# A short first token list and a first expert that begins with 32 tokens, in a two-layer decoder step

## The chip, the cores and the metric

The kernel runs on one core of a Trainium2 chip. The metric is the time of one execution on the device, in microseconds (us). Engines are called PE (matmul), DVE (vector), ACT (activation), POOL and SP; the last two mostly issue DMAs here. PE's clock is granted at one of two levels, 1.2 or 2.4 GHz; the profile writes them as 0.50 and 1.00.

## What is computed

One inference step of a trunk with two layers, over 512 prompt tokens and 64 sample tokens (576 rows of 1024 values). Each layer is a mixer (convolution and attention in layer 0, sparse attention in layer 1) followed by a mixture of 16 experts. The change touches the experts' part alone. Cut to that part:

```python
def hier_moe(h, w_group, b_group, w_router, b_router, w_gate, w_up, w_down):
    g_w, g_idx = lax.top_k(jax.nn.softmax(g_logits, axis=-1), 1)      # one group of four
    top_v, top_i = lax.top_k(e_in, TOP_K_INNER)                       # two experts inside it
    expert_id = g_idx * E_PER_GROUP + top_i
    ...
    for e in range(N_EXPERTS):
        hid = jax.nn.silu(x2 @ w_gate[e]) * (x2 @ w_up[e])
        y = y + combine[:, e:e + 1] * (hid @ w_down[e])
```

Each token goes to 2 of 16 experts; an expert's three matrices are 1024x512, 1024x512 and 512x1024 values of 4 bytes, so 2 MB each.

## The kernel before

**Slots and parts.** The experts are worked in 16 slots. Slots 0 and 1 always hold experts 0 and 1; the others are handed out by how many tokens each expert got. `UNITS` gives each slot's room in units of 32 tokens, 47 units in all. A slot is cut into parts (`PARTS`) of 64 tokens, with a last one of 32 where the number of units is odd. Slot 0 has 3 units: part 0 has 64 tokens, part 1 has 32. A part's place in the sequence is called g. For each g, PE does gate and up (L1306, function `part_features`) and, one part later, down (L1326) of g-1.

**Routing.** After the mixer's output projection, DVE works out each token's expert from the router's scores (`route`, L2109 on). It waits for the scores (`route_mm`), sets `quarter` with four memsets (L2111), finds the two experts of each token, and gives PE a 0/1 mask. PE adds up the places of the tokens in their experts' lists (L1268, L1271, `pos_mm`), and DVE reduces these to `pos_of` (L2154), ten numbers for each partition. Then come the lists: DVE compares `pos_of` with the slot numbers 0 to 127 (`slot_of`, two instructions of 128x640), PE multiplies this by the token numbers (L1277), DVE copies the result to `list16` (L2159), PE spreads the lists of experts 0 and 1 over the partitions (L1281), and DVE writes the row numbers to `tok_u` (L2163). `pos_x` and `slot_x` (a compare of 128x320) serve the places 128 to 159 of a list (L1285). Behind this stand, on DVE and in this order, the rank of the experts (`ranking`, whose last instruction L2174 tells SP which weights to load), the order of the other lists (`list_order`, ending with L2202), and then `inputs(0)`.

**Gathers.** POOL fetches tokens by an indirect DMA for each unit of 32 tokens (L855) from `hn_scratch`, a copy of the normalised rows in DRAM, which POOL itself wrote a little earlier (L780). It waits for the `tok` semaphore and for that copy. `inputs(g)` on DVE turns the gathered rows (L2280) and multiplies them by the gain (L1892, a helper's line that stands for most two-operand instructions). PE waits for this (`xgt`) at the start of each part.

**Weights.** SP streams 48 blocks of 2 MB a layer (L578) into a ring of 7 (layer 0) or 8 (layer 1) places. The first 6 are loaded earlier. From slot 2 on each load waits for `ranked` once, and then for the place that it overwrites: `gate_mm`, `up_mm` or `down_mm` of an earlier slot's last part. ACT issues the DMAs that store each part's output.

## Time and profile before

| | us |
|---|---|
| median of 3 runs | 1408.08 (1398.65 to 1408.93) |
| the profiled execution | 1394.93 |
| its span, first to last instruction | 1393.2 |
| mean granted clock of PE | 0.952 of full |
| PE busy | 1257.5 (90%) |
| DVE busy | 688.6 (49%) |
| ACT busy | 304.7 (22%) |
| POOL busy | 246.7 (18%) |
| mean DMA traffic | 245 GB/s |

The profile is of one execution. 1.7 us of its time lie outside the span. The experts' part of layer 0 runs from about 392 to 660 us, that of layer 1 from about 1096 to 1359 us.

### The profile page before, as it was taken

Reading aid. Unit: us, or ns where it says so; the run is one execution under the profiler, and the core shown is the slowest. Engines: PE = TensorE matmul, PEld = TensorE weight load, DVE = VectorE, ACT = ScalarE, POOL = GpSimd, SP = SyncE. Lnnn points to the kernel's source line nnn. Section 1 sums busy time; section 2 is a strip of 40 time slices with the busy share of each in tenths; the row PEclk is TensorE's granted clock in tenths of the full one; section 3 lists DMA queues with packets and bytes.
Section 4 is the critical chain, followed back from the end, with each engine's and each line's share of the span. In section 5 each row is a group of like instructions: output and inputs, shape, how many; then the busy total and the mean of one; then the engine's idle time right before and its main releaser. Section 6 shows DMA issues by size and latency. Waiting matters only on the chain. (4 is left out here: it accounts for less than half of the span.)

```text
span 1393.2 us, 26984 instructions
## 1 busy us (share of the span) xinstructions
PE 1257.5 (90%) x10555; PEld 705.8 (51%) x10556; DVE 688.6 (49%) x1763; ACT 304.7 (22%) x783; POOL 246.7 (18%) x537
## 2 busy tenths in 40 slices
PE   7999999999779999889599999999999599999890
PEld 3444446554455556455444444555645365555550
DVE  2139954452546443222547897676314645433225
ACT  2121134421201011001213213566602100110012
POOL 1010065001031112100301664000010312111102
PEclk9999999999889999999699998999999799999995
DMA  9443459964479999999501131333342899999966
GB/s 295 144 147 114 155 187 328 333 231 155 167 274 346 393 424 424 424 423 406 164 5 61 35 121 61 122 123 123 126 167 100 310 361 354 425 425 423 422 281 214
DMA packets 88558, 341.05 MB, mean 245 GB/s; under 512 B 26803, under 2 KB 34067, under 8 KB 74466
## 3 DMA queue, kind: packets, MB, share of 16 engines
q1 hardware_dynamic: 67466, 289.49, 54.1%
q0 software_dynamic: 11616, 37.56, 7.5%
q10 hardware_dynamic: 9344, 12.20, 2.5%
q8 instruction: 88, 1.44, 0.4%
q14 instruction: 44, 0.36, 0.1%
HBM read 309.09 MB, written 30.47 MB: 244 GB/s over the span
## 5 line engine op out<-in xcount | busy, mean ns | idle before, releaser
L1306 PE MATMUL banks<-arena 128*32 128x128 f32 (+1 forms) x4736 | 346.5, 333 | 25.5 <-issue 18.2
L1306 PEld LDWEIGHTS banks<-arena 128*32 128x32 f32 (+1 forms) x4736 | 241.9, 126 | 141.4 <-issue 52.8
L1892 DVE TENSOR_TENSOR arena<-arena,banks 128x256 f32<-128x256 f32 (+5 forms) x84 | 38.4, 458 | 382.1 <-PE banks L1306 289.3
L1326 PE MATMUL banks<-arena 128*64 128x512 f32 (+1 forms) x1184 | 173.3, 492 | 1.8 <-ACT arena L1786 1.6
L855 POOL DMA_INDIRECT arena<-hn_scratch,arena x94 | 90.5, 963 | 363.9 <-DVE arena L1892 323.0
L988 PE MATMUL banks<-arena 128*128 128x512 f32 x320 | 142.9, 601 | 0.4 <-DMA arena<-in_wstream 0.4
L1216 PE MATMUL banks<-arena 128*128 128x512 f32 x256 | 114.3, 602 | 3.6 <-ACT arena L1826 2.2
L1016 PE MATMUL banks<-arena 128*128 128x512 f32 x256 | 116.5, 600 | 0.0
L1892 DVE TENSOR_TENSOR arena<-arena 128x256 f32<-128x256 f32 (+13 forms) x220 | 91.1, 433 | 36.5 <-ACT arena L1637 18.2
L1326 PEld LDWEIGHTS banks<-arena 128*64 128x64 f32 (+1 forms) x1184 | 59.8, 124 | 90.3 <-issue 78.5
L1786 ACT ACTIVATE arena<-banks 128x512 f32<-128x512 f32 (+1 forms) x56 | 29.6, 528 | 303.4 <-PE banks L1326 303.4
L988 PEld LDWEIGHTS banks<-arena 128*128 128x128 f32 x320 | 60.2, 193 | 70.2 <-issue 69.8
L2292 DVE STREAM_TRANSPOSE arena<-arena 32x128 f32<-32x128 f32 x304 | 92.0, 303 | 4.9
L2454 DVE SCALAR_TENSOR_TENSOR arena<-arena 128x512 f32<-128x512 f32 x120 | 82.1, 747 | 1.0
L1216 PEld LDWEIGHTS banks<-arena 128*128 128x128 f32 x256 | 48.4, 193 | 62.8 <-issue 59.0
L1892 DVE TENSOR_TENSOR arena<-banks,arena 128x128 f32<-128x128 f32 (+3 forms) x91 | 38.0, 438 | 82.1 <-ACT arena L1708 69.1
L1016 PEld LDWEIGHTS banks<-arena 128*128 128x128 f32 x256 | 46.7, 190 | 56.1 <-issue 54.5
L1796 ACT ACTIVATE arena<-banks 128x256 f32<-128x256 f32 (+1 forms) x56 | 19.6, 349 | 197.4 <-PE banks L1306 191.9
L1574 ACT ACTIVATE arena<-arena 128x1024 f32<-128x1024 f32 (+1 forms) x25 | 26.4, 1056 | 147.8 <-DVE arena L1892 101.7
L1691 ACT ACTIVATE arena<-arena 128x128 f32<-128x128 f32 (+3 forms) x96 | 53.0, 557 | 8.0 <-DVE arena L1938 7.9
L1938 DVE CUSTOM_DVE_ANT_0 arena<-banks,arena 128x128 f32<-128x128 f32 (+3 forms) x96 | 42.7, 482 | 11.4 <-PE banks L1044 7.4
L932 PE MATMUL banks<-arena 128*128 128x128 f32 (+1 forms) x160 | 23.3, 296 | 26.7 <-DVE arena L2348 18.1
(298 smaller groups left out, 1374.7 us busy)
## 6 DMA issues: line engine op xcount, KB each, us to landing
arena<-in_wstream SPq DMA_DIRECT2D x109, 2048.0 KB, 17.2
arena<-in_fox_kt SPq DMA_DIRECT2D x64, 256.0 KB, 4.5
arena<-in_fox_v SPq DMA_DIRECT2D x64, 256.0 KB, 4.2
arena<-in_dsa_page SPq DMA_DIRECT2D x64, 256.0 KB, 4.1
expert_rows<-arena ACTq DMA_DIRECT2D x76, 128.0 KB, 9.4
expert_rows<-arena POOLq DMA_DIRECT2D x1, 6656.0 KB, 19.6
hn_scratch<-arena POOLq DMA_DIRECT2D x8, 512.0 KB, 3.0
expert_rows<-arena ACTq DMA_DIRECT2D x68, 32.0 KB, 7.6
```

The costliest lines, as they stand in the source:

```text
L855: pool.indirect_dma_start(xg[s % 2][:, 256 * w:256 * w + 256], None, rows4, bass.IndirectOffsetOnAxis(tok_u[:, w, s:s + 1], 0))\
L988: last = mm(bank(job % 4), xt[:, c, c0:c1], w[:, c, :], start=(c == 0), stop=(c == DC - 1))
L1016: last = mm(bank(job % 2), xt[:, c, c0:c1], w[:, c, :], start=(c == 0), stop=(c == DC - 1))
L1216: last = mm(bank(out_bank(l, job)), xt[:, c, c0:c1], w[:, c, :], start=(c == first), stop=(c == end))
L1306: last = mm(g3(bank(b, 0, 4 * n, n * j, n * j + n), 4), x[:, c, :], g3(w[:, c, :], 4)[:, :, n * j:n * j + n], start=(c == 0), stop=(c == D ...
L1326: last = mm(bank(3, 0, 8 * n, n * q, n * q + n), ht2[g % 2][:, n * c:n * c + n], w[:, c, 8 * n * q:8 * n * q + 8 * n], start=(c == 0), sto ...
L1691: af(x, x, ACT.Exp, bias=mx[:, c:c + 1], scale=-1.0, accum_out=esum[:, c:c + 1])\
L1786: af(y2[i][:, 0:8 * n], bank(3, 0, 8 * n), ACT.Copy).then_inc(S(f"y_ev{l}"), 1)
L1892: return v.tensor_tensor(out, x, y, op)
L1938: v.tensor_tensor_reduce(sbp[j % 2][a][:, 0:n], bank(a, 0, n), bias(t), -1.0, -TAKEN, ALU.add, ALU.min, mx[:, c:c + 1]).then_inc(S(f"sb{l} ...
L2292: last = v.transpose(g3(ht2[g % 2][p:p + 32, :], 4)[:, :, 32 * half:32 * half + 32], g3(hid2[g % 2][r:r + 32, :], 4)[:, :, 32 * par:32 * p ...
L2454: last = v.scalar_tensor_tensor(out=op, in0=ip, scalar=w, in1=op, op0=ALU.mult, op1=ALU.add)
```

## The change

In words: `CUTS` gives slot 0 the parts of 32 and then 64 tokens; every other slot keeps its parts. A short list, places 0 to 31 of the experts 0 and 1, is made ahead of the whole lists, with a `slot_x` compare of its own, and `tok_u` of the first unit is written from it. POOL waits for the first unit's row numbers and then, separately, for the second's. The four memsets of `quarter` stand behind the mask, and `key` and `pos_x` stand between the steps of the short list.

```diff
-PARTS = tuple((s, 64 * i, min(64, 32 * UNITS[s] - 64 * i)) for s in range(NE) for i in range((UNITS[s] + 1) // 2))
+CUTS = tuple(((0, 1), (1, 2)) if s == 0 else tuple((2 * i, min(2, UNITS[s] - 2 * i)) for i in range((UNITS[s] + 1) // 2))
+             for s in range(NE))
+PARTS = tuple((s, 32 * first, 32 * n) for s in range(NE) for first, n in CUTS[s])
...
+def part_with(s, unit):
+
+    return max(j for j, (first, _) in enumerate(CUTS[s]) if first <= unit)
...
             for s in range(NE):
-                if s in (0, 2):
-                    pool.wait_ge(S(f"tok{l}"), upto(f"tok{l}", s + 2))
+                if s == 2:
+                    pool.wait_ge(S(f"tok{l}"), upto(f"tok{l}", 6))
                 for w in range(UNITS[s]):
+                    if s == 0 and w < 2:
+                        pool.wait_ge(S(f"tok{l}"), upto(f"tok{l}", 2 * w + 2))
                     pool.indirect_dma_start(xg[s % 2][:, 256 * w:256 * w + 256], None, rows4,
...
+            pe.wait_ge(S(f"placed{l}"), upto(f"placed{l}", 1))
+            for n in range(2 * NT):
+                last = mm(bank(5, 0, NE, 0, 32), slot_x[:, n, :], tok_of[:, n, :], start=(n == 0), stop=(n == 2 * NT - 1))
+            last.then_inc(S(f"list_mm{l}"), 1)
+            pe.wait_ge(S(f"tok{l}"), upto(f"tok{l}", 1))
+            mm(bank(6, 0, 2), spread[0:32, 0], list16[0:32, 0:2], start=True, stop=True).then_inc(S(f"list_mm{l}"), 1)
...
-            for w in range(3):
+            for w in range(1, 3):
                 last = mm(bank(6, 2 * w, 2 * w + 2), spread[:, w], list16[:, 0:2], start=True, stop=True)
...
             dve.wait_ge(S(f"tables{l}"), upto(f"tables{l}", 1))
-            for q in range(4):
-                v.memset(quarter[32 * q:32 * q + 32], float(q))
             dve.wait_ge(S(f"route_mm{l}"), upto(f"route_mm{l}", 1))
...
+            tt(slot_x, bc_mid(slot16[:, 0:32], 2 * NT), bc_last(pos_of, 32), ALU.is_equal).then_inc(S(f"placed{l}"), 1)
+            step(v.scalar_tensor_tensor(out=key, in0=cnt, scalar=16.0, in1=kofs, op0=ALU.mult, op1=ALU.add))
+            dve.wait_ge(S(f"list_mm{l}"), upto(f"list_mm{l}", 1))
+            v.tensor_copy(list16[0:32, 0:2], bank(5, 0, 2, 0, 32)).then_inc(S(f"tok{l}"), 1)
+            step(v.tensor_scalar(pos_x, pos_of, -float(CAP), None, ALU.add))
+            dve.wait_ge(S(f"list_mm{l}"), upto(f"list_mm{l}", 2))
+            v.tensor_scalar(tok_u[:, 0, 0:2], bank(6, 0, 2), 4.0, quarter, ALU.mult, ALU.add)\
+                .then_inc(S(f"tok{l}"), 1)
```

How the order of the engines moves. DVE in layer 0, from the reduction to `pos_of` to the one to the rank's first half, before:

```order
L2154 TENSOR_REDUCE arena<-arena 128x10 [waits dve_chain]
L1892 TENSOR_TENSOR arena<-arena 128x640 [waits dve_chain]
L1892 TENSOR_TENSOR arena<-arena 128x640
L2159 CAST arena<-banks 128x16 [waits list_mm]
L2160 TENSOR_SCALAR arena<-arena 128x10
L1892 TENSOR_TENSOR arena<-arena 128x320 [waits dve_chain]
L2163 TENSOR_SCALAR arena<-banks,arena 128x3x2 [waits list_mm]
L2165 SCALAR_TENSOR_TENSOR arena<-arena 128x16
L1892 TENSOR_TENSOR arena<-arena 128x256 [waits dve_chain]
```

The same stretch with the change, where the helper's line is L1908:

```order
L2170 TENSOR_REDUCE arena<-arena 128x10 [waits dve_chain]
L1908 TENSOR_TENSOR arena<-arena 128x320 [waits dve_chain]
L2172 SCALAR_TENSOR_TENSOR arena<-arena 128x16
L2174 CAST arena<-banks 32x2 [waits list_mm,dve_chain]
L2175 TENSOR_SCALAR arena<-arena 128x10
L2177 TENSOR_SCALAR arena<-banks,arena 128x2 [waits list_mm,dve_chain]
L1908 TENSOR_TENSOR arena<-arena 128x640 x2
L2183 CAST arena<-banks 128x16 [waits list_mm]
L1908 TENSOR_TENSOR arena<-arena 128x320
L2186 TENSOR_SCALAR arena<-banks,arena 128x2x2 [waits list_mm]
L1908 TENSOR_TENSOR arena<-arena 128x256
```

The two long compares (128x640) and everything behind them now stand behind a compare, two waits for PE and two small instructions.

PE in layer 0, from the lists to the first expert's matmuls, before:

```order
L1277 MATMUL banks<-arena 128x16 [waits placed]
L1277 MATMUL banks<-arena 128x16 x4
L1281 MATMUL banks<-arena 128x2 [waits tok]
L1281 MATMUL banks<-arena 128x2 x2
L1285 MATMUL banks<-arena 32x16 [waits placed]
L1285 MATMUL banks<-arena 32x16 x9
L1290 MATMUL banks<-arena 128x14 [waits tok]
L1290 MATMUL banks<-arena 128x14 x3
L1291 MATMUL banks<-arena 128x1
L1306 MATMUL banks<-arena 64x256 [waits weights_0,xgt]
```

The same stretch with the change:

```order
L1285 MATMUL banks<-arena 32x16 [waits placed]
L1285 MATMUL banks<-arena 32x16 x9
L1288 MATMUL banks<-arena 128x2 [waits tok]
L1293 MATMUL banks<-arena 128x16 [waits placed]
L1293 MATMUL banks<-arena 128x16 x4
L1293 MATMUL banks<-arena 128x16 [waits placed]
L1293 MATMUL banks<-arena 128x16 x4
L1297 MATMUL banks<-arena 128x2 [waits tok]
L1297 MATMUL banks<-arena 128x2
...
L1307 MATMUL banks<-arena 128x1
L1322 MATMUL banks<-arena 32x128 [waits weights_0,xgt]
```

The short list's eleven matmuls stand first, and the first expert's matmuls are of the 32-token form.

## Rows read from the trace of the kernel before

**Rows 1.** Timeline of layer 0, PE: start us, us, engine, line, what, [idle before <- releaser]

```profile
392.26 12.46 PE L1306 MATMUL banks<-arena 128*64 128x256 f32 x192 [2.17 <-DVE arena L1892]
...
408.14 7.08 PE L1306 MATMUL banks<-arena 128*64 128x256 f32 x64
...
416.89 3.68 PE L1306 MATMUL banks<-arena 128*32 128x128 f32 x128
...
570.36 5.08 PE L1306 MATMUL banks<-arena 128*64 128x256 f32 x32 [5.44 <-issue]
```

**Rows 2.** Windows: us, busy PE, PEld, DVE, ACT, POOL; clock, DMA share, GB/s

```profile
399.00:400.00 1.00, 1.00 (x12) 0.69 (x10) 0.14 (x1) 0.00 (x0) 0.70 (x1) 1.00 0.00 0
459.00:460.00 1.00, 1.00 (x15) 0.49 (x8) 0.94 (x4) 0.38 (x1) 0.00 (x0) 1.00 0.14 57
470.00:655.00 185.00, 172.56 (x1978) 102.46 (x1976) 61.56 (x165) 16.90 (x38) 23.02 (x24) 0.97 1.01 424
```

**Rows 3.** Timeline of layer 0, SP's queue

```profile
389.14 0.35 SPq L578 DMA_DIRECT2D arena<-in_wstream  x1
403.19 0.34 SPq L578 DMA_DIRECT2D arena<-in_wstream  x1
```

**Rows 4.** Timeline of layer 0, the first gathers and inputs

```profile
386.66 1.04 POOL L855 DMA_INDIRECT arena<-hn_scratch,arena  x1 [10.75 <-DVE arena L2163]
...
388.00 0.98 POOL L855 DMA_INDIRECT arena<-hn_scratch,arena  x1 [0.30 <-issue]
...
389.29 0.95 POOL L855 DMA_INDIRECT arena<-hn_scratch,arena  x1 [0.30 <-issue]
...
390.77 0.71 DVE L2280 STREAM_TRANSPOSE arena<-arena 128x512 f32<-128x512 f32 x1 [1.13 <-DMA arena<-hn_scratch,arena]
...
397.10 0.45 DVE L2280 STREAM_TRANSPOSE arena<-arena 128x256 f32<-128x256 f32 x1 [4.58 <-DMA arena<-hn_scratch,arena]
397.57 0.43 DVE L1892 TENSOR_TENSOR arena<-arena 128x256 f32<-128x256 f32 x1
```

**Rows 5.** Timeline of layer 1, the same places

```profile
1090.95 1.02 POOL L855 DMA_INDIRECT arena<-hn_scratch,arena  x1 [10.67 <-DMA hn_scratch<-arena]
...
1095.02 0.71 DVE L2280 STREAM_TRANSPOSE arena<-arena 128x512 f32<-128x512 f32 x1 [1.04 <-DMA arena<-hn_scratch,arena]
...
1096.51 13.60 PE L1306 MATMUL banks<-arena 128*64 128x256 f32 x192 [2.09 <-DVE arena L1892]
```

**Rows 6.** Timeline of layer 0, the start of the routing on DVE

```profile
374.34 0.70 PE L958 MATMUL banks<-arena 128*128 128x20 f32 x4
...
375.03 0.37 DVE L2111 MEMSET arena<- 32x1 f32 x4
375.41 0.24 DVE L1892 TENSOR_TENSOR arena<-banks,arena 128x80 f32<-128x80 f32 x1
```

**Rows 7.** Timeline of layer 0, the lists

```profile
381.84 0.24 DVE L2150 COPY arena<-banks 128x80 f32<-128x80 f32 x1 [0.56 <-PE banks L1271]
...
382.91 1.56 DVE L1892 TENSOR_TENSOR arena<-arena 128x640 f16<-128x640 f16 x2
...
384.86 0.17 DVE L2159 CAST arena<-banks 128x16 f16<-128x16 f32 x1 [0.40 <-PE banks L1277]
...
385.09 0.24 PE L1281 MATMUL banks<-arena 128*128 128x2 f16 x3 [0.27 <-DVE arena L2159]
385.15 0.49 DVE L1892 TENSOR_TENSOR arena<-arena 128x320 f16<-128x320 f16 x1
385.56 0.22 DVE L2163 TENSOR_SCALAR arena<-banks,arena 128x6 uint32<-128x6 f32 x1
...
385.69 0.16 DVE L2165 SCALAR_TENSOR_TENSOR arena<-arena 128x16 f32<-128x16 f32 x1
385.69 0.44 PE L1285 MATMUL banks<-arena 128*32 128x16 f16 x10 [0.36 <-DVE arena L1892]
385.89 0.42 DVE L1892 TENSOR_TENSOR arena<-arena 128x256 f32<-128x256 f32 x1
```

More of the change, by code:

```diff
@@ L68, in part_units @@
 def part_units(s, j):
-    return max(0, min(2, UNITS[s] - 2 * j))
+    return CUTS[s][j][1] if j < len(CUTS[s]) else 0
+def part_with(s, unit):
+    return max(j for j, (first, _) in enumerate(CUTS[s]) if first <= unit)
 ENDS = tuple(sum((u + 1) // 2 for u in UNITS[:s + 1]) for s in range(NE))
@@ L122 @@
     (1, "route_mm mask pos_mm ranked tables turns row_u qbd"),
-    (4, "tok list_mm"),
-    (3, "placed"),
+    (6, "tok list_mm"),
+    (4, "placed"),
     (2, "tail_mm tail_ev route_dve route_act"),
@@ L1287, in route @@
             last.then_inc(S(f"list_mm{l}"), 1)
-            pe.wait_ge(S(f"tok{l}"), upto(f"tok{l}", 3))
+            pe.wait_ge(S(f"tok{l}"), upto(f"tok{l}", 5))
             for w in range(4):
@@ L2148, in route @@
                tokid16[:, 0:NT].unsqueeze(1).unsqueeze(3).broadcast_to([128, 2, NT, NE]), ALU.mult)
+            for q in range(4):
+                v.memset(quarter[32 * q:32 * q + 32], float(q))
             dve.wait_ge(S(f"pos_mm{l}"), upto(f"pos_mm{l}", 1))
@@ L2157, in route @@
                    ALU.is_equal).then_inc(S(f"placed{l}"), 1)
-            dve.wait_ge(S(f"list_mm{l}"), upto(f"list_mm{l}", 1))
+            dve.wait_ge(S(f"list_mm{l}"), upto(f"list_mm{l}", 3))
             v.tensor_copy(list16, bank(5, 0, NE)).then_inc(S(f"tok{l}"), 1)
-            step(v.tensor_scalar(pos_x, pos_of, -float(CAP), None, ALU.add))
             tt(slot_x, bc_mid(slot16[:, 0:32], 2 * NT), bc_last(pos_x, 32), ALU.is_equal).then_inc(S(f"placed{l}"), 1)
-            dve.wait_ge(S(f"list_mm{l}"), upto(f"list_mm{l}", 2))
-            v.tensor_scalar(tok_u[:, 0:3, 0:2], g3(bank(6, 0, 6), 3), 4.0, quarter, ALU.mult, ALU.add)\
+            dve.wait_ge(S(f"list_mm{l}"), upto(f"list_mm{l}", 4))
+            v.tensor_scalar(tok_u[:, 1:3, 0:2], g3(bank(6, 2, 6), 2), 4.0, quarter, ALU.mult, ALU.add)\
                 .then_inc(S(f"tok{l}"), 1)
-            step(v.scalar_tensor_tensor(out=key, in0=cnt, scalar=16.0, in1=kofs, op0=ALU.mult, op1=ALU.add))
             step(tt(g3(square, NE), bc_mid(key, NE), bc_last(key, NE), ALU.is_gt))
@@ L2198, in list_order @@
             v.tensor_copy(order16[:, 0:14], tok_s[:, 0:14])
-            dve.wait_ge(S(f"list_mm{l}"), upto(f"list_mm{l}", 3))
+            dve.wait_ge(S(f"list_mm{l}"), upto(f"list_mm{l}", 5))
             step(tt(tok_x[0:32, :], chosen[0:32, 2, :], bank(7, 0, NE, 0, 32), ALU.mult))
@@ L2204, in other_tokens @@
         def other_tokens(l):
-            dve.wait_ge(S(f"list_mm{l}"), upto(f"list_mm{l}", 4))
+            dve.wait_ge(S(f"list_mm{l}"), upto(f"list_mm{l}", 6))
             v.tensor_scalar(tok_u[:, 4, 2:3], bank(4, 56, 57), 4.0, quarter, ALU.mult, ALU.add)
@@ L2274, in inputs @@
             def inputs(g):
-                s, j = PART_OF[g]
-                n = 32 * part_units(s, j)
+                (s, j), (_, off, n) = PART_OF[g], PARTS[g]
                 name, count = gathered(l, s, j)
                 dve.wait_ge(S(name), upto(name, count))
-                x = xgt[s % 2][:, :, 64 * j:64 * j + n]
-                step(v.transpose(x.rearrange("p c (w i) -> p w c i", i=32), xg[s % 2][:, 512 * j:512 * j + 8 * n]))
+                x = xgt[s % 2][:, :, off:off + n]
+                step(v.transpose(x.rearrange("p c (w i) -> p w c i", i=32), xg[s % 2][:, 8 * off:8 * off + 8 * n]))
                 tt(x, x, bc_last(gain[2 * l + 1], n), ALU.mult).then_inc(S(f"xgt{l}"), 1)
```

8 lines of the change are left out of this document (4 added, 4 removed).

## The prediction

> **What bounds the kernel now.** I read the timeline of PE through the experts of layer 0 first, then the windows of DMA, SP's queue, and last the timeline where the experts start. PE works without a gap from 392.26 us on for most of the phase; a part of 64 tokens takes 7.08 us for gate and up, one of 32 takes 3.68 us, so the time goes with the tokens [rows 1]. Late in the phase PE waits for weights, once for 5.44 us, and comes back slower: 32 matmuls take 5.08 us where half of 7.08, or 3.54, is normal [rows 1]. The windows tell when the weights' stream falls behind. The reader is to see the two empty stretches: no traffic at all at 399 us and a share of 0.14 at 459 us [rows 2]. There the stream had nothing to load, because every place in the ring still held weights that PE needed. From 470 to 655 us, in one window, the DMA share is full [rows 2]. So the end of the phase is set by DMA, but the moment from which DMA runs without rest is set by PE, which frees the places; SP's loads show the same, one at 389.14 us and the next at 403.19, when the first slot's last gate is done [rows 3]. A change of PE's start therefore reaches the end of the layer in full, and a change of the stream's start does not, as long as it is less than the empty time.
>
> What sets PE's start is the chain at the head: DVE ends the order of lists (L2202) 1.13 us ahead of 390.77, so at 389.64, waits for the second gather, transposes at 390.77, multiplies, and PE starts at 392.26 [rows 4]. Layer 1 is alike, with a wait of 1.04 us from 1093.98 to 1095.02, and PE at 1096.51 [rows 5]. So two things have to be early for PE: the gathers that the first part needs, and DVE's way to the end of L2202. The change hastens the first and burdens the second.
>
> **The memsets.** The scores are ready at 375.04, and DVE's memsets run from 375.03 to 375.40; the first work on the scores starts at 375.41 [rows 6]. Without them it can start at about 375.10, so everything behind gains 0.3 us. At their new place they take the same 0.37 us, and DVE waits 0.56 us there for PE's sums [rows 7], which hides them. Without that cover they would cost what they gave.
>
> **The short list.** It stands in front of the whole lists, so its round trip between DVE and PE is paid by all that follows. From the rows of the lists: the compare to PE's first matmul 0.54 us (385.15 to 385.69), PE's ten matmuls 0.44, to DVE's copy 0.04, from the copy to PE's spread 0.23 (384.86 to 385.09), the spread at most 0.24, to `tok_u` 0.04, and 0.13 until the next DVE instruction starts (385.56 to 385.69) [rows 7]. That is 1.66 us. Two small instructions that stood behind now run inside the waits: `pos_x`, 0.2 us between the copy's start and the compare, and `key` (L2165), 0.2 us to the square [rows 7]. Net 1.66 - 0.4 = 1.26 us later, less the memsets' 0.3: about 0.95 us later for the ranking, for the weights' stream, and for L2202. Queued behind this on DVE are the whole lists, the ranking, the order of the lists and both first inputs; PE, POOL and SP wait for them.
>
> **The gathers.** The first row numbers are written about 0.54 + 0.44 + 0.04 + 0.23 + 0.24 + 0.04 + 0.22 = 1.75 us after the compare's start, and that start is 382.91 - 0.3: 384.4. POOL started 0.88 us after L2163's end (385.78 to 386.66) [rows 4, 7], so the first gather starts at about 385.2 in layer 0, where it was 386.66. The second gather was seen by DVE 2.77 us after its start (388.00 to 390.77) [rows 4]; with that the first has landed at 388.0. In layer 1 POOL waited for the copy of the rows, not for the list [rows 5], so the first gather cannot go before about 1090.9 and lands at about 1093.7. The second gather's row numbers now come from the longer way: 385.78 + 0.95 = 386.7, plus 0.88 is 387.6, where it was 388.00; the third then starts near 388.9 instead of 389.29. Nearly unchanged.
>
> **Where the first part starts.** In layer 0 DVE is through with L2202 at 389.64 + 0.95 = 390.6 and the gather has long landed; the wait of 1.13 us goes, and DVE's own work takes its place. In layer 1 it is 1093.98 + 0.95 = 1094.9, again behind the gather. So the inputs start 0.2 us and 0.1 us earlier than before. They are half as large: 0.45 + 0.43 with the small gap is 0.90 us (397.10 to 398.00), against 1.49 us from 390.77 to PE's start, which for the small form is 0.96 with the same 0.06 us hand-over [rows 4]. That is 0.53 us. Sum: 0.7 us earlier in layer 0, 0.65 in layer 1, or 1.35 us in all.
>
> **The second part.** It now needs two gathers and 64 tokens of work on DVE. If the third gather lands 2.8 us after 388.9, at 391.7, the inputs are done at 393.2. PE has 3.68 us of work in the first part at full clock, and more here, since it starts at the low level. The first 192 matmuls took 12.46 us and 13.60 us, where 7.08 + 3.68 = 10.76 is the full-speed time [rows 1, 5]. The excess of 1.70 and 2.84 us is half of the time spent at 1.2 GHz, so the low clock held 3.4 us in layer 0 and 5.7 us in layer 1. A first part of 32 tokens then ends 3.68 + 1.7 = 5.4 us after its start, at about 397.0, almost 4 us after its successor is ready. The new order of sizes costs PE nothing: 32 and 64 tokens make 10.76 us as 64 and 32 did. The first gate place comes free 1.7 us sooner by the sizes alone, 3.4 us of small work ahead of the long gate instead of 6.8 ahead of the short one. That only moves a load into an empty stretch [rows 2, 3]. ACT issues four stores and then two, where it was two and then four.
>
> **The clock.** An earlier start gains in full only if the clock rises earlier by as much. If the rise stays where it is, 0.7 us more at 1.2 GHz is worth 0.35 us. Between the layers the low stretch differs by 2.3 us, worth 1.14 us. I take the full gain, since a later or earlier rise is as likely, and keep 0.35 us a layer for one end and 0.65 + 1.14 = 1.8 us a layer for the other: 0.7 to 3.6 us in all.
>
> **A rule to weigh.** The third gather, started at 389.29 just behind a weights' load at 389.14, was seen by DVE at 397.10, 7.8 us later, while the second, 1.1 us ahead of the load, took 2.8 [rows 3, 4]. With the change the third starts at 388.9 and the load at 389.14 + 0.95 = 390.1, so 1.2 us ahead; I take the short time. The Trainium skill (DMA: Bandwidth & Descriptors, Queues, rings and completion order) says that each DMA engine goes round between its queues packet by packet. By that rule a gather of 128 KB would get a share beside any load and would not wait for the block; this trace speaks against an equal share. By the rule the rival below would have no price at all.
>
> **The rivals.** *The third gather is late after all.* It lands 7.8 us after its start, at 396.7, the 64 tokens take 1.43 us, and the second part is ready at 398.1, 1.1 us after the first ends. Less 0.7 us gained it is +0.4 in layer 0; in layer 1 the third gather starts 2.6 us behind the first at 1090.95, lands at 1101.3 and makes the part ready at 1102.8, while the first part, with 2.84 us of excess, ends at 1095.9 + 6.5 = 1102.4: a wait of 0.4, or -0.25 in all [rows 5]. Together +0.15 us: no change. For it: 1.2 us is a thin lead. Against it: the second gather had the same lead. *Slower: the gap holds the clock down.* The same late gather, and the gap while PE is still at the low level delays the rise; after 5.44 us without work the clock cost 1.54 us on the next 32 matmuls [rows 1]. Adding that to each layer gives 0.15 + 3.1 = +3.3 us. It decides from the point where the third gather lands later than about 395.5. *Slower: the stream.* If the loads were bound from their start, 0.95 us a layer would come on top of the gains' loss, +1.9 us. The empty second at 399 us speaks against it [rows 2]. *The change does nothing:* DVE or the gathers turn out as late as before, since the short list in front costs what it gives; 0.0 us.
>
> **How the numbers follow.** Chances: forecast 0.55 (-0.7 to -3.6 us, likeliest -1.35); nothing gained, by the late gather or by the cost of the list, 0.25; held clock 0.12 (+3.3); the stream 0.08 (+1.9). On the profiled execution the sum gives 1394.93 - 1.35 = 1393.6. The median shown is 13.2 us above that execution, and the three runs spread over 10.3 us, much more than any case here. I carry the difference to the median: 1408.08 - 1.35 = 1406.7. The range has to hold this spread: the profiled execution and one run stand at 1395 and 1399, two at 1408 and 1409. From 1394.93 to 1408.93 + 3.3, cut a little at the upper end, is 1395 to 1411. About 1% (14 us) is what a measurement of this kernel can tell from no change. No case comes near it; 0.02 each way is left for what the runs' own spread can do, 0.96 for the same.
>
> **What would show it.** Right: the first work on the scores at once behind PE's end; POOL's first gather of layer 0 some 1.4 us earlier and that of layer 1 not; L2202's counterpart about 0.95 us later; no wait of DVE for the first gather; PE's first expert matmul 0.7 us earlier against the routing's start, in the 32-token form; no gap before the second part; the ring's empty stretch near 459 us still there. Wrong: a gap of PE before the second part, a low clock held beyond 6 us, or a first input that starts later than 390.8 by the old count. What would make the time wrong, with every step right, is the runs' own spread, which is larger than the edit.

## The result, and the profile after

| | before | after |
|---|---|---|
| median of 20 runs | 1403.43 us (1398.65 to 1409.27) | 1409.53 us (1405.09 to 1412.97) |
| the profiled execution, its span | 1394.93, 1393.2 | 1411.95, 1410.0 |

The ratio is 1.0039, with an interval of 1.0027 to 1.0050: the change cost 6.1 us, where the forecast was 1.35 us less. One thing has to be said ahead of all that follows. The kernels were timed in several sessions, always side by side with the kernel before, and that kernel itself has two levels: 1393 us in two sessions, 1403 to 1406 in the others. Its profiled execution of 1394.93 us, which stands ahead of the prediction, is of the lower level; the 20 runs beside it are mostly of the upper one. So the two profiles are not of the same kind, and their difference of 16.8 us is not the change's. Two executions of the kernel before, beside experiments 13 to 15, took 1708 and 3299 us; no ratio uses them.

**The head, as forecast.** Timeline of DVE after, layer 0; it answers to [rows 4, 6, 7].

```profile
374.56 0.24 DVE L1908 TENSOR_TENSOR arena<-banks,arena 128x80 f32<-128x80 f32 x1
...
380.38 0.35 DVE L2164 MEMSET arena<- 32x1 f32 x4
381.00 0.24 DVE L2166 COPY arena<-banks 128x80 f32<-128x80 f32 x1 [0.26 <-PE banks L1280]
...
383.15 0.15 DVE L2174 CAST arena<-banks 32x2 f16<-32x2 f32 x1 [0.51 <-PE banks L1285]
...
383.65 0.22 DVE L2177 TENSOR_SCALAR arena<-banks,arena 128x2 uint32<-128x2 f32 x1 [0.27 <-PE banks L1288]
...
389.95 0.14 DVE L2224 CAST arena<-arena 32x1 f16<-32x1 f32 x1
390.02 0.42 DVE L2301 STREAM_TRANSPOSE arena<-arena 128x256 f32<-128x256 f32 x1
...
391.13 0.70 DVE L2301 STREAM_TRANSPOSE arena<-arena 128x512 f32<-128x512 f32 x1
```

The memsets are hidden: DVE's wait for PE's sums is 0.26 us where it was 0.56. The waits of the short list (0.51 and 0.27 us) are there. The list order ends at 390.09 and both inputs start without any wait, also the second, whose third gather was late before [rows 4].

**The part that broke.** Timeline of PE, layer 0 and then layer 1; it answers to [rows 1, 5].

```profile
390.95 5.39 PE L1322 MATMUL banks<-arena 128*32 128x128 f32 x68 [0.42 <-DVE arena L1908]
396.71 0.43 PE L1322 MATMUL banks<-arena 128*32 128x128 f32 x5 [0.36 <-issue]
398.16 0.41 PE L1322 MATMUL banks<-arena 128*32 128x128 f32 x4 [1.03 <-issue]
399.58 1.10 PE L1322 MATMUL banks<-arena 128*32 128x128 f32 x5 [1.00 <-issue]
401.02 9.54 PE L1322 MATMUL banks<-arena 128*32 128x128 f32 x110 [0.35 <-issue]
410.48 1.93 PE L1342 MATMUL banks<-arena 128*32 128x256 f32 x32
412.35 7.13 PE L1322 MATMUL banks<-arena 128*64 128x256 f32 x64
...
1102.76 3.62 PE L1322 MATMUL banks<-arena 128*32 128x128 f32 x46 [0.42 <-issue]
1107.22 0.43 PE L1322 MATMUL banks<-arena 128*32 128x128 f32 x5 [0.85 <-issue]
1108.65 0.44 PE L1322 MATMUL banks<-arena 128*32 128x128 f32 x5 [1.00 <-issue]
```

PE has its inputs and its weights, and waits for nothing that the profile shows ("issue"), yet four or five matmuls go out, then a second passes, and again. The rows begin 1.42 to 1.45 us apart (396.71, 398.16, 399.58, 401.02). I call these the small steps. The first part is 128 matmuls of the 32-token form; together with the 64 of the second part they are the 192 that stood in one row before [rows 1]. From PE's start to the third part's gate, which I call the head from here on, it is 390.95 to 412.35, or 21.40 us; in layer 1 it is 22.66. Before's profile has 392.26 to 408.14, 15.88 us [rows 1]. The first row hides the beginning: 57 of its 68 matmuls start within 3.3 us, the other 11 from 394.54 on at the pace of the steps.

POOL's queue in the same stretch:

```profile
384.75 1.49 POOL L864 DMA_INDIRECT arena<-hn_scratch,arena  x1 [9.44 <-DVE arena L2177]
...
393.69 0.95 POOL L864 DMA_INDIRECT arena<-hn_scratch,arena  x1 [0.30 <-issue]
...
398.71 0.95 POOL L864 DMA_INDIRECT arena<-hn_scratch,arena  x1 [0.30 <-issue]
```

Eleven gathers run one behind the other, to 399.66 (not all are shown). The last five are slot 2's. They wait for slot 0's second input, which is 6.0 us earlier than before (391.13 against 397.10 [rows 4]), so they are in the queue early as well, and they lie beside the 32-token part.

Windows of after (us; busy PE, PEld, DVE, ACT, POOL; clock; DMA share; GB/s), one inside the steps and one behind them:

```profile
397.00:398.00 1.00, 0.13 (x4) 0.00 (x0) 0.00 (x0) 0.00 (x0) 0.69 (x2) 1.00 0.82 320
402.00:403.00 1.00, 1.00 (x28) 1.00 (x23) 0.00 (x0) 0.00 (x0) 0.00 (x0) 0.50 0.00 0
```

Four matmuls in a microsecond at the full clock; and when PE runs again its clock has fallen to the lower level, so the steps are paid a second time: 28 matmuls of this form in the microsecond, where the run of experiment 16 has 24 at the lower level (window 393 to 394 us) and 42 at the full one (394 to 395).

### The profile page after: what moved, and what is told of

The parts are those of the page before. It is cut to its first block and busy times, and to the rows that moved or that the text cites. A ratio compares the mean times of both kernels' runs of the same rounds, so it can differ in the third digit from the quotient of the medians.

```text
span 1410.0 us, 27036 instructions
## 1 busy us (share of the span) xinstructions
PE 1266.4 (90%) x10575; PEld 710.0 (50%) x10576; DVE 689.6 (49%) x1769; ACT 304.6 (22%) x783; POOL 248.3 (18%) x537
## 3 DMA queue, kind: packets, MB, share of 16 engines
q8 instruction: 88, 1.44, 0.4%
## 5 line engine op out<-in xcount | busy, mean ns | idle before, releaser
L1322 PE MATMUL banks<-arena 128*32 128x128 f32 (+1 forms) x4736 | 357.1, 338 | 32.1 <-issue 27.1
L1322 PEld LDWEIGHTS banks<-arena 128*32 128x32 f32 (+1 forms) x4736 | 247.5, 128 | 153.1 <-issue 67.2
L1908 DVE TENSOR_TENSOR arena<-arena,banks 128x256 f32<-128x256 f32 (+5 forms) x84 | 38.5, 459 | 411.7 <-PE banks L1322 299.7
L1908 DVE TENSOR_TENSOR arena<-arena 128x256 f32<-128x256 f32 (+16 forms) x222 | 92.1, 433 | 36.4 <-ACT arena L1653 18.2
L1908 DVE TENSOR_TENSOR arena<-banks,arena 128x128 f32<-128x128 f32 (+3 forms) x91 | 38.1, 438 | 81.5 <-ACT arena L1724 69.0
L941 PE MATMUL banks<-arena 128*128 128x128 f32 (+1 forms) x160 | 23.4, 296 | 25.7 <-DVE arena L2369 16.7
```

The costliest lines, as they stand in the source:

```text
L1322: last = mm(g3(bank(b, 0, 4 * n, n * j, n * j + n), 4), x[:, c, :], g3(w[:, c, :], 4)[:, :, n * j:n * j + n], start=(c == 0), stop=(c == D ...
L1908: return v.tensor_tensor(out, x, y, op)
```

## The experiments

The medians of before by session: 1393.24 us (35 runs; the first four kernels), 1405.58 (23; the next four, on the same chip), 1404.76 (13), 1404.14 (12), 1393.23 (25; the last three). Ratios are to the kernel before of the same session. Heads are given for layer 0 and layer 1, from the one profile of each run. A kernel that begins with 32 tokens has a head 1.6 us shorter by the count alone, since a down of 32 tokens lies in it and not one of 64: from the down's start to that of the next part it is 1.87 us (410.48 to 412.35 in after) and not 3.49 (404.65 to 408.14 in before).

**1. The short list without the cut.**

```diff
-CUTS = tuple(((0, 1), (1, 2)) if s == 0 else ...
+CUTS = tuple(((0, 2), (2, 1)) if s == 0 else ...
```

> The changed kernel with slot 0 cut as 64 and 32 tokens again; the short list, its waits and the moved memsets stay. In the changed kernel's trace PE starts the first expert on time but works the 32-token form of the first part in steps of 0.7 and 1.4 us from about 394 to 401 us, and the same in layer 1. Theory 1 (the form of the first part is at fault: 32-token matmuls are four times as many instructions per us as the 64-token ones, and they meet the start of the weights' stream): no steps here, PE's first expert starts within 0.5 us of before, and the whole stands within 2 us of the kernel before. Theory 2 (the short list is at fault, by what it does to the order of list, gathers and stream): the steps stay, and the whole is 5 us slower than before.

Measured: 0.9979 (0.9962 to 0.9997), 1390.16 us; heads 16.36 and 16.46, no steps.

**2. The cut without the short list** (the kernel before with slot 0 in 32 and 64 tokens; memsets and lists as before).

> The kernel before with slot 0 cut as 32 and then 64 tokens, and no short list. Theory 1 (form of the first part): the steps of 0.7 and 1.4 us stand in the first part of both layers, some 5 us are lost in each head, and the whole is about 5 us slower than before. Theory 2 (the short list): no steps, and since the first inputs are 0.5 us smaller while the gathers are as before, the whole is 0 to 2 us faster than before.

Measured: 1.0043 (1.0021 to 1.0065), 1398.38 us. No steps, but the wait for the late third gather is real. PE in this kernel, layer 0:

```profile
392.14 5.75 PE L1313 MATMUL banks<-arena 128*32 128x128 f32 x128 [1.48 <-DVE arena L1899]
400.45 7.13 PE L1313 MATMUL banks<-arena 128*64 128x256 f32 x64 [2.56 <-DVE arena L1899]
```

The third gather starts at 389.88, behind the stream's load of 389.73, and PE waits 2.56 us for the second part. In layer 1 it starts 0.08 us ahead of the load (1094.31 and 1094.39), and PE waits 4.64 us. This is the first rival of the prediction, and without the short list it comes true. The first part took 5.75 us, close to the 5.4 of the forecast.

**3. The stream held.** The whole change, and SP's loads from slot 2 on wait until the first part's up matmuls are done:

```diff
+            sp.wait_ge(S(f"up_mm{l}"), upto(f"up_mm{l}", 1))
```

> The changed kernel, with one wait more on SP: the weights of slot 2 and later are not loaded before PE is done with the up product of the first part (up_mm of g 0). Theory 1a (PE's instructions or operands come late because the weights' stream fills the DMA engines): the steps vanish, the first part takes 5.4 to 6.6 us, and PE reaches the third part some 5 us sooner in each layer than in the changed kernel; the whole is 3 to 8 us faster than the changed kernel. Theory 1b (the form stalls by itself right after an idle PE, or because of the gathers): the steps stay as they are.

Measured: 0.9984 (0.9965 to 1.0003), 1392.17 us; heads 15.27 and 14.32, no steps.

**4. The gathers held.** The whole change, and POOL waits before slot 1's gathers:

```diff
+                if s == 1:
+                    pool.wait_ge(S(f"up_mm{l}"), upto(f"up_mm{l}", 1))
```

> The changed kernel, with one wait more on POOL: the gathers of slot 1 and later are not issued before PE is done with the up product of the first part. Theory 1a (weights' stream): the steps stay, and the whole is as slow as the changed kernel. Theory 1c (the gathers and POOL's writing of their descriptors hold PE up): the steps vanish and the first part takes 5.4 to 6.6 us in both layers.

Measured: 0.9991 (0.9973 to 1.0010), 1391.71 us; heads 14.95 and 15.43, no steps (in layer 1, PE waits 1.19 us for slot 1's held input). At this point both holds seemed to cure the kernel, and I took the steps for the work of stream and gathers together. The last session shows that three and four prove nothing of the kind: they were made where no kernel had steps.

**5. The memsets alone**, in the kernel before.

> The kernel before with the four memsets of quarter moved behind the mask, and nothing else. The first work on the router's scores starts right behind PE's end instead of 0.37 us later, in both layers; the memsets stand in DVE's wait for pos_mm. Worth 0.6 us in all, or a ratio of 0.9996: not to be told from 1 by the times, so the trace of the head decides. A rival: the memsets end behind PE's sums at their new place and cost there what they gave.

Measured: 0.9974 (0.9959 to 0.9988), 1402.06 us, in a session of the upper level. The gain of 3.5 us is far more than the 0.3 us a layer that the memsets take; I have no cause for the rest, and no run was made for it. Its profile has steps in both layers, in the 32-token part, which here is the second: heads 19.76 and 22.45. So the steps aren't the changed kernel's alone.

**6. Slot 2's gathers held** in the whole change, behind the wait for the row numbers:

```diff
                 if s == 2:
                     pool.wait_ge(S(f"tok{l}"), upto(f"tok{l}", 6))
+                    pool.wait_ge(S(f"up_mm{l}"), upto(f"up_mm{l}", 1))
```

> The changed kernel, with the five gathers of slot 2 held on POOL until PE is done with the up product of the first part; the gathers of slots 0 and 1 and the weights' stream go as in the changed kernel. Holding the gathers of slots 1 and 2, or holding the stream, took the steps away. Theory 3 (the steps need POOL's gathers, the stream and the 32-token form at once, and those gathers are slot 2's, which the early second part lets start while PE is still in the first): no steps, the first part takes 5.4 to 6.6 us, the whole is 2 to 5 us faster than before. Rival (slot 1's gathers are enough): the steps stay.

Measured: 0.9941 (0.9918 to 0.9963), 1398.10 us; heads 15.95 and 14.99. No steps but one pause of 0.7 us. PE in layer 0:

```profile
392.59 5.86 PE L1323 MATMUL banks<-arena 128*32 128x128 f32 x126 [0.42 <-DVE arena L1909]
399.13 7.46 PE L1323 MATMUL banks<-arena 128*32 128x128 f32 x66 [0.68 <-issue]
```

**7. The cut, with the stream behind the third gather**: kernel 2, and SP waits for the first input.

```diff
+            sp.wait_ge(S(f"xgt{l}"), upto(f"xgt{l}", 1))
```

> The kernel before with slot 0 cut as 32 and 64 tokens, no short list, and the weights' stream held until DVE has made the first part's inputs. Without that hold PE had no steps but waited 2.6 and 4.6 us for the third gather, which was issued within 0.2 us of the stream's first load. Theory 3: the third gather now lands early, the wait for the second part goes, slot 2's gathers come early too, and the steps appear in its place, 4 to 6 us in each layer; no gain over the cut alone. Rival (the short list has a share in the steps): no wait and no steps, and the whole is 3 us faster than before.

Measured: 1.0040 (1.0021 to 1.0059), 1410.04 us. The third gather is early and its wait is gone, and the steps are there, the longest of all: heads 25.03 and 23.55. The short list isn't needed for them: here too the second input, and so slot 2's gathers, come early.

**8. Slot 2's gathers as plain DMAs.** The whole change; the five indirect gathers of slot 2 are replaced by plain transfers of the same size from the start of the rows, on the same queue, so slot 2 computes with other tokens than its own:

```diff
+                    if s == 2:
+                        pool.dma_start(xg[s % 2][:, 256 * w:256 * w + 256], rows4[0:128, :])\
+                            .then_inc(S(gathered(l, s, part_with(s, w))[0]), 16)
+                        continue
```

> The changed kernel with the five gathers of slot 2 replaced by plain DMAs of POOL with the same bytes to the same place (the first 128 rows of the source for each, so slot 2 computes with other tokens than its own). If the traffic of these transfers beside the stream is what slows PE, the steps stay as they are. If it is POOL's work on indirect gathers, the steps vanish or end within 3 us.

Measured: 0.9917 (0.9886 to 0.9947), 1393.68 us; heads 15.80 and 14.34, no steps. POOL and PE in layer 0:

```profile
393.33 2.78 POOL L865 DMA_DIRECT2D arena<-hn_scratch  x5
...
390.91 14.01 PE L1326 MATMUL banks<-arena 128*32 128x128 f32 x192 [0.42 <-DVE arena L1912]
```

The same bytes in the same stretch, beside the same stream, do no harm, in a session where before stood at 1405.58 and where kernels 5 and 7 had steps. What goes with the steps is the indirect gather, 0.95 us of POOL each (five take 6.0 us, the plain ones 2.78), not the amount of traffic. Whether it is POOL's own work, or the packets that such a gather makes, this run doesn't separate.

**9 and 14. The kernel before, profiled again, twice.**

> The kernel before, run once more with a profile. The length looked at is that of the head: from PE's first matmul of the experts to the start of the third part's gate; it was 15.88 and 17.02 us in the profile of before. If the small steps (4 to 8 matmuls per 0.7 or 1.4 us) belong to every kernel whose 32-token part meets slot 2's gathers and the weights' stream, before has them too in some executions, in its second part, as the kernel with the memsets alone had (19.76 and 22.45 us): then this profile shows a head of 18 to 22 us in at least one layer. If they come only where the short part stands first, the head is 16 to 17 us again, without steps.

> The kernel before, a third profile. The first had no steps (15.88 and 17.02 us from PE's first expert matmul to the third part's gate), the second had them in both layers (22.51 and 20.29 us). If steps are the rule and the first profile was a rare one, 19 to 23 us in both layers again; if it is half and half, at least one layer is near 16.

Measured: 1405.1 and 1402.53 us, and steps in both layers of both: heads 22.51 and 20.29, then 20.86 and 21.79. PE, POOL and two windows of kernel 9, layer 0:

```profile
391.14 10.94 PE L1306 MATMUL banks<-arena 128*64 128x256 f32 x109 [2.27 <-DVE arena L1892]
402.23 0.42 PE L1306 MATMUL banks<-arena 128*32 128x128 f32 x3
402.98 0.27 PE L1306 MATMUL banks<-arena 128*32 128x128 f32 x1 [0.33 <-issue]
403.70 0.41 PE L1306 MATMUL banks<-arena 128*32 128x128 f32 x3 [0.45 <-issue]
405.13 0.43 PE L1306 MATMUL banks<-arena 128*32 128x128 f32 x4 [1.02 <-issue]
406.58 3.66 PE L1306 MATMUL banks<-arena 128*32 128x128 f32 x72 [1.02 <-issue]
...
399.42 0.95 POOL L855 DMA_INDIRECT arena<-hn_scratch,arena  x1 [6.25 <-DVE arena L1892]
...
404.47 0.96 POOL L855 DMA_INDIRECT arena<-hn_scratch,arena  x1 [0.30 <-issue]
...
399.00:400.00 1.00, 1.00 (x12) 0.67 (x10) 0.69 (x4) 0.00 (x0) 0.58 (x1) 1.00 0.00 0
404.00:405.00 1.00, 0.11 (x2) 0.11 (x1) 0.96 (x2) 0.00 (x0) 0.69 (x2) 1.00 0.22 70
```

From 402 to 406 us only the gathers' queue moves anything (70 GB/s at 404 us), and at 404 PE gets out two matmuls in a microsecond. So the stream isn't needed, which corrects the theory of experiment 3. The first profile of before, at 1393.2 us, had the same five gathers from 398.75 on beside the same 32-token part at the full clock, without a step. Between those spans, 1403.3 and 1393.2, lie 10.1 us; the heads of the two profiles differ by 6.6 and 3.3, together 9.9 us. In experiment 14 the heads differ by 9.8 us and the spans by only 7.5. So the steps in the heads make up about the difference between the two levels of the kernel before.

**10, 11 and 12. Three kernels in which slot 2's gathers don't meet the short part.** Kernel 10 is kernel 5 with the hold, 11 is kernel 1 with it, both until the second part's up matmuls; 12 is kernel 6 again.

> The kernel before with the memsets moved, and POOL's gathers for slot 2 held until the up matmuls of the second part are done, so that they meet no 32-token part. Theory (the steps cost time in before as well): no steps in either layer, head of 15.5 to 16.5 us, and 0.993 to 0.996 of before, that is a good deal less than the 0.9974 of the memsets alone. Rival (only the changed kernel, with its short part first, is hurt by the gathers): 0.997 to 0.998 as with the memsets alone. Second rival (the hold makes slot 2's first part wait for its gathers): a gap of PE ahead of the third part of over 1 us, and 1.000 or more.

> The changed kernel with slot 0 cut into 64 and 32 tokens as before, and slot 2's gathers held until the second part's up matmuls are done. It differs from the kernel with the memsets moved and the same hold by the short list alone, which makes everything behind it about 1.3 us later and the first gather earlier. Theory: the stream's later start costs nothing, PE's start is about the same or up to 0.4 us later: within 0.002 of that kernel. Rival (the stream's start counts): 1.3 us a layer, 0.002 above it or more.

> The whole change, with slot 2's gathers held until the first part's up matmuls are done, once more, beside the two held kernels without the new cut on the same chip. If the early first part is worth what was forecast once the steps are gone (1.35 us, 0.001), it stands 0.001 to 0.003 below the kernel with the short list and the hold; if the change is worth nothing beyond the hold and the memsets, the three are equal within 0.001; the earlier ratio to before was 0.9941.

Measured: 0.9930 (0.9906 to 0.9954), 0.9925 (0.9896 to 0.9953), 0.9926 (0.9899 to 0.9952); medians 1395.66, 1395.00, 1395.53. No steps in any of the six heads (16.2 and 15.8; 16.0 and 16.7; 16.2 and 16.6), but one pause of 0.6 us in kernel 12, where kernel 6 had its own. PE in kernel 10, layer 0:

```profile
389.74 12.81 PE L1308 MATMUL banks<-arena 128*64 128x256 f32 x192 [2.31 <-DVE arena L1894]
```

The hold brings all three to within 2.5 us of the lower level, and with it the short list and the cut are worth nothing that shows: the three are equal within 0.0005. The gain of the early start, 0.001, is smaller than these intervals.

**13. The changed kernel, profiled again.**

> The changed kernel once more with a profile. Its first profile had steps in the 32-token first part of both layers, with 21.40 and 22.66 us from PE's first expert matmul to the third part's gate. If the early gathers of slot 2 make the steps a fixture of the changed kernel, both layers show them again, 20 to 24 us each. If they come by chance in it as they seem to in the kernel before (none in its first profile, both layers in its second), one layer or both are free of them, at 15 to 17 us.

Measured: 1412.17 us (one execution), steps in both layers, heads 22.84 and 23.14.

**15. The whole change with the longer hold.**

> The whole change, with slot 2's gathers held until the second part's up matmuls are done, as in the two held kernels that begin with 64 tokens. If the steps were all that kept the change from its forecast 1.35 us, it stands at 0.9915 to 0.992 of before, 0.001 below those two (0.993 and 0.9925). If the change is worth nothing by itself, it is equal to them within 0.001. If the hold is now too long for slot 2 (its part comes 1.5 us sooner, since the long down matmuls stand behind the third gate), PE waits for it and the ratio is 0.994 or more.

Measured: 0.9974 (0.9961 to 0.9986), 1400.20 us, 0.005 worse than kernel 12. The first two parts are free of steps (one pause of 0.4 us), but the third, of 64 tokens, isn't. PE and POOL in layer 0:

```profile
412.66 0.66 PE L1323 MATMUL banks<-arena 128*64 128x256 f32 x4 [0.17 <-issue]
414.10 0.66 PE L1323 MATMUL banks<-arena 128*64 128x256 f32 x4 [0.77 <-issue]
415.54 0.81 PE L1323 MATMUL banks<-arena 128*64 128x256 f32 x5 [0.78 <-issue]
...
406.92 0.95 POOL L865 DMA_INDIRECT arena<-hn_scratch,arena  x1 [12.10 <-PE banks L1323]
...
414.47 0.95 POOL L865 DMA_INDIRECT arena<-hn_scratch,arena  x1 [0.30 <-issue]
```

The held gathers of slot 2 meet those of slot 3 in one unbroken train, and 5.7 us into it the steps begin, four or five matmuls per 1.44 us again. So the 64-token form can be hurt too: the part takes 10.6 us. But the train alone doesn't decide it. Kernels 10 and 11 have the same seven gathers in one train beside the same part (403.3 to 411.9 and 405.9 to 414.5 us in layer 0), and there it takes 8.0 and 7.9 us, with a single pause of 0.35. What makes the difference is open. The third expectation had the size of the loss, for another reason: PE doesn't wait for its gathers, it starves beside them.

**16, 17 and 18. The changed kernel timed, kernel 3 and kernel 1 again, in one session.**

> The changed kernel once more, timed beside the two kernels that follow and the kernel before on one chip. In one session the kernel before stood at 1393 us, in all others at 1404 to 1406. If the small steps in the 32-token part belong to the changed kernel in every session, it stands at 1409 to 1413 us with steps in both layers whatever the kernel before does; if a session can be free of steps for all kernels, both stand near 1392 to 1395.

> The changed kernel with the weights' stream held until the first part's up matmuls are done, once more, in a session in which the kernel before is timed again. If the stream is needed for the steps, none are seen, and the ratio to before is 0.990 to 0.994 where before stands at 1404. If POOL's train of gathers makes the steps by itself (the second look at the kernel before showed them at a time without any stream), they are back: a head of 20 to 24 us, and a ratio of 1.000 to 1.005; the first run of this kernel was then only a session without steps.

> The changed kernel with slot 0 cut into 64 and 32 tokens as before, without any hold, once more. Slot 2's gathers then run while PE is in the 64-token form, and end before the 32-token part begins. If only the 32-token form is hurt, there are no steps, the head is 16 to 17 us, and the ratio is that of the held kernels, 0.9925 to 0.994, where before stands at 1404. If the gathers hurt either form, or if the hold itself gave something, 0.997 to 1.000.

Measured, with before at 1393.23 us: the changed kernel 0.9978 (0.9954 to 1.0002), 1389.60 us; stream held 0.9988 (0.9965 to 1.0011); list alone 0.9989 (0.9972 to 1.0007). No steps anywhere. The changed kernel of experiment 16, PE, POOL and SP's queue, layer 0:

```profile
389.11 13.62 PE L1322 MATMUL banks<-arena 128*32 128x128 f32 x192 [0.41 <-DVE arena L1908]
402.66 1.93 PE L1342 MATMUL banks<-arena 128*32 128x256 f32 x32
404.52 7.13 PE L1322 MATMUL banks<-arena 128*64 128x256 f32 x64
...
391.84 0.95 POOL L864 DMA_INDIRECT arena<-hn_scratch,arena  x1 [0.30 <-issue]
...
396.87 0.96 POOL L864 DMA_INDIRECT arena<-hn_scratch,arena  x1 [0.31 <-issue]
...
387.91 15.33 SPq L585 DMA_DIRECT2D arena<-in_wstream  x3
```

The same program that had steps in two sessions runs through here, with the same train of eleven gathers and the same stream beside the same matmuls. The heads are 15.41 and 15.33 us.

**A mark of the two levels outside the head.** The third part of 32 tokens (it starts at about 438 to 452 us in layer 0, 1140 to 1163 in layer 1) runs at the full clock in every kernel here, with two indirect gathers beside its end that no experiment moved. PE in layer 1 of kernel 8 and then of the changed kernel of experiment 16:

```profile
1147.57 3.48 PE L1326 MATMUL banks<-arena 128*32 128x128 f32 x119
1151.28 0.43 PE L1326 MATMUL banks<-arena 128*32 128x128 f32 x3 [0.24 <-issue]
...
1143.68 3.72 PE L1322 MATMUL banks<-arena 128*32 128x128 f32 x128
```

Its 128 matmuls take 5.6 us in kernel 8 and 3.7 in the other. In the eight profiles of the lower level (the first of before, kernels 1 to 4, 16 to 18) it is 3.7 to 3.8 us in 15 of 16 places and 4.2 in one; in the twelve of the upper level (the first of the changed kernel, 5 to 15) it is 4.2 to 5.6 us in 22 of 24, whether the head has steps or not. In the other two (layer 0 of kernels 10 and 13) it is 3.7, and there the second gather starts only behind the part's end. So kernels 6, 8, 10, 11, 12 and 15 were profiled in executions in which PE could be hurt, and their heads were free all the same. It also says that the level isn't a matter of the head alone.

## Why the prediction was wrong

**What held.** The memsets gave 0.3 us and were hidden. The short list put the end of the list order later, counted from the reduction to `pos_of`: 8.38 us after (381.71 to 390.09), against 7.08 before (382.55 to 389.63), so 1.30 us; the forecast was 1.26. Counted from the end of the scores, the first gather of layer 0 was 1.3 us early (10.30 us and not 11.62), that of layer 1 waited for the copy of the rows. DVE waited for no gather. From the end of the scores PE's start is 16.50 us instead of 17.22 in layer 0 and 0.61 us earlier in layer 1; the forecast was 0.7 and 0.65. The third gather was early, so the likeliest rival fell, and no gap stood before the second part. The stream's first load came 1.6 us later, not 0.95, and cost nothing: the held stream of kernel 3 starts 7.3 us behind PE's start (396.01 against 388.68), in after 0.8 us ahead of it, and the kernels 3 and 17 are not slower than the kernel before.

**The step that failed.** "A first part of 32 tokens then ends 3.68 + 1.7 = 5.4 us after its start, at about 397.0, almost 4 us after its successor is ready." Its 128 matmuls took 12.5 us in layer 0 and 13.8 in layer 1 (390.95 to 403.50, 1102.76 to 1116.57). I had priced the 32-token form by a row in which it runs free, late in the phase, and had asked of POOL's gathers only when they land, not what they lie beside. The prediction had the second input done at 393.2, where it was 398.0 before; slot 2's five gathers wait for that input alone, and so it also followed that they move onto the 32-token part. In the kernel before they met the 32-token part too, which made its upper level, but the train was of five gathers that began while PE was still in the 64-token form (399.42 in kernel 9, its steps from 402.2 to 406.6, 4.4 us). In the changed kernel the train is of eleven, and the steps run from 394.5 to 401.0 in layer 0, 6.5 us, and from 1105.0 to 1112.9 in layer 1, 7.9 us. That the longer train makes the longer steps is my reading; no run varied its length alone.

**The sum in the sessions with steps.** Heads of before are 22.51, 20.29, 20.86 and 21.79, mean 21.4; those of the changed kernel 21.40, 22.66, 22.84 and 23.14, mean 22.5, or 24.1 with the 1.6 us of the down. That is 2.7 us a layer more, less 0.7 for the earlier start, so 2.0 a layer or 4.0 us in all, of the 6.1 measured. Most of the remaining 2 us can be seen in the profiles. Near the end of layer 0's experts PE stands idle once more (after):

```profile
661.73 0.41 PE L1322 MATMUL banks<-arena 128*32 128x128 f32 x4 [1.52 <-issue]
```

A wait of 0.9 to 1.9 us ahead of the last four gate and up matmuls of layer 0 stands in all 13 profiles of kernels with the short list, at either level, and in none of the seven without it. In each of the 13 a packet of an instruction queue starts 2.3 to 2.6 us before PE goes on (queue q8, one packet of 16 KB, at 659.3 in after). It may be that the edit moved the border between two blocks of instructions to this place; no run tested it. The third part of 32 tokens, by contrast, costs the changed kernel only 0.3 us more than before (sums of 10.5 and 8.8 us for its two profiles, 8.6 and 10.1 for kernels 9 and 14).

**The sum in a session without.** There the changed kernel is 3.6 us faster, with an interval from 6.4 us faster to 0.3 slower. The forecast of 1.35 lies in it, and so does no change at all, so this does not confirm the forecast. The first part took 6.6 us there (6.5 in layer 1), 1.2 and 1.1 more than the 5.4 forecast. The kernel with the short list alone is as fast within the error (0.9979 and 0.9989). So that the cut gives anything is not shown in any session.

**The rivals.** None of the four was what happened. "Slower: the gap holds the clock down" came nearest in size (+3.3 us) and was right in that PE, when it starves at the beginning of the experts, loses its clock; but its cause, a late third gather, wasn't there. That cause is real in kernel 2, which is 0.43% slower than before.

**Two slips of reading.** The first part's gate and up, which stand ahead of slot 0's last gate, take 3.68 us with the change and 7.08 before [rows 1], not 3.4 and 6.8; the last gate is done 1.70 us sooner all the same, (7.08 + 1.84) - (3.68 + 3.54). And the wait of 5.44 us was called one for weights, but its row names "issue"; the profile shows no releaser for it.

**The base.** The prediction saw that the profile lay 13 us below the median and called it the runs' own spread. It was the profile of another level of the kernel, with no steps in it, and so the one thing that mattered couldn't be seen in it. The sign was there: the profiled time, 1394.93, lay below all three runs. The measured 1409.53 us lies inside the stated range of 1395 to 1411, but that is luck: the range had been widened for the spread of the runs, which was the two levels. Against the kernel before, the change went the other way.

**What stays open.** Shown is that the steps go with POOL's indirect gathers: in the sessions of the upper level no head had a run of steps where slot 2's were kept off the 32-token part or made plain transfers (kernels 6, 8, 10, 11, 12 and 15, twelve heads, three of them with one pause of 0.4 to 0.7 us), and all twelve heads had them where the gathers lay beside it (the changed kernel's first profile, 5, 7, 9, 13 and 14). Not shown is why two sessions had none in any head; the chip isn't the reason, since experiments 1 to 4 and 5 to 8 were on the same one and lay on different levels. Nor is it shown what PE lacks. It may be instructions: the steps are mostly of three to five matmuls with their weight loads, in the 32-token form as in the 64-token form. And ACT's first activation came at 401.15 in after, 4.8 us behind the end of the PE row that holds the gate's 64 matmuls (390.95 + 5.39 = 396.34), with its releaser unknown; the steps end at 401.02. The DMA queues of after, from 396.5 to 401.5 us:

```profile
q0 software_dynamic: 314, 0.83, 47.5%
q1 hardware_dynamic: 30, 0.23, 10.9%
```

No packet of an instruction queue starts in this stretch of layer 0 (the nearest start at 395.3 and 403.3), which speaks against a new block of instructions that is late; in layer 1 one does, at 1107.5, and the steps go on for 5 us behind it. The Trainium skill (Runtime: NRT & Kernel Launch, Instruction fetch mechanics) says that the fetch of instructions is hidden behind their issue; by that rule the steps could not come from the fetch. If they are a matter of instructions at all, these traces disagree with it beside a train of indirect gathers.

## What to carry to other kernels

When an edit makes a step early, follow also what waits for that step alone: here an earlier input released five gathers onto the part in which PE starts the most matmuls per microsecond (128 in 3.68 us, where the 64-token form has 64 in 7.08). A profile whose time lies at the edge of the runs is of another kind than the median until shown otherwise; a second profile of the unchanged kernel would have shown it here. And where one queue's work hurts PE, a single wait that moves it may be worth more than the edit under study: 0.7% here in the sessions of the upper level. At the lower level the hold itself was not timed; the nearest kernel, 4, stood at 0.9991 (0.9973 to 1.0010).

## What the hardware showed that I had not expected

- PE in steps of mostly three to five matmuls per 0.72 or 1.43 us, with the full clock granted (1.00 at 397 to 398 us in after, 404 to 405 in kernel 9), beside a train of POOL's indirect gathers of 0.95 us each; not beside five plain DMAs of the same bytes issued in 2.78 us.
- The same program, with the same transfers at the same times, had steps in some sessions and none in others: 1409.5 and 1389.6 us for the changed kernel, 1403 to 1406 and 1393 us for the kernel before, with both levels on one chip for the kernel before. The third part of 32 tokens tells the level from a single profile: 3.7 us or 4.2 to 5.6 in 37 of 40 places.
- An indirect gather took 1.49 us of POOL instead of 1.04 when it ran beside DVE's compare of 128x640 (384.75).
- A gather that starts 0.15 us behind a load of 2 MB (389.88 and 389.73 in kernel 2) kept PE waiting 2.56 us, and one that starts 0.08 us ahead of it 4.64 us (1094.31 and 1094.39), while in after, with the third gather 2.1 us ahead (387.99 and 390.13), DVE found it landed.
- A wait of 0.9 to 1.9 us for PE ahead of four matmuls near the end of layer 0, in the 13 profiles with the short list alone, each time 2.3 to 2.6 us behind the start of a 16 KB packet of an instruction queue.
